# A hybrid decoder layer on one core: x's first 256 columns fetched alone, the first two units by k tiles, the gate weights rounded two units sooner, and one delta order turned

## The reference

```
xn   = RMSNorm(x);  proj = xn @ W_in          (7 x 1024 columns and 16 gate columns b, a)
A    = gated delta rule, 8 heads: conv of 4 taps + SiLU on q, k, v; L2 norm of q, k;
       g = -exp(A_log) softplus(a + dt_bias), beta = sigmoid(b); chunks; RMSNorm * SiLU(z)
B    = block attention, 8 heads, RMSNorm of q and k, causal softmax over the block of 256 keys
h    = x + concat(A, B) @ W_o
h    = h + (silu(RMSNorm(h) @ W_gate) * (RMSNorm(h) @ W_up)) @ W_down       (width 5632)
out  = h + sigmoid(RMSNorm(h) @ W_pg) * (p @ W_pp)                          (p is 256 x 256)
```

## Time and profile before

| | |
|---|---|
| median of three runs | 1342.83 us |
| profiled execution, time / span | 1343.03 us / 1341.0 us |
| DVE busy | 790.0 us (59%) |
| ACT busy | 626.1 us (47%) |
| POOL busy | 53.0 us (4%) |
| matmuls | 6796 |
| DMA, mean | 178 GB/s |

### The profile page before, as it was taken

One profiled execution on the slowest core, in us unless ns is written; L12 is line 12 of the kernel. 1 busy time (PEld: TensorE's weight loads), 2 busy tenths in 40 slices (PEclk: granted clock), 3 DMA queues, 4 the chain that ended last, 5 costly groups with the idle time before them and its releaser, 6 DMA issues.

```text
span 1341.0 us, 18239 instructions
## 1 busy us (share of the span) xinstructions
PE 1333.0 (99%) x6796; PEld 1102.6 (82%) x6796; DVE 790.0 (59%) x987; ACT 626.1 (47%) x785; POOL 53.0 (4%) x71
## 2 busy tenths in 40 slices
PE   9999999999999999999999999999999999999998
PEld 8788888887888888888888888888888888888887
DVE  6578885788586555555555555455555555555554
ACT  6477443543465545444444443344444444444643
POOL 4002000230000000000000000000000000000000
PEclk9999999999999999999999999999999999999999
DMA  8555554455434565666666656666666665555554
GB/s 265 161 170 173 149 150 125 144 153 148 140 120 150 175 194 178 201 190 188 187 189 191 186 189 194 194 191 195 191 194 186 188 189 188 185 189 189 187 192 141
DMA packets 125929, 238.35 MB, mean 178 GB/s; under 512 B 9695, under 2 KB 10258, under 8 KB 125866
## 3 DMA queue, kind: packets, MB, share of 16 engines
q1 hardware_dynamic: 125866, 237.48, 57.9%
HBM read 235.36 MB, written 2.10 MB: 177 GB/s over the span
## 4 chain that ended last, share of the span: by engine, by line
PE 97%; DVE 0%; ACT 0%; issue 0%; DVEq 0%
PE pair L550 30%; PE pair L552 29%; PE pair L551 29%; PE bg L667 2%; PE bg L732 2%; PE bg L815 1%; PE bg L607 1%; PE bg L585 0%; PE bg L713 0%; PE pair L885 0%; PE pair L883 0%; PE pair L884 0%; PE bg L631 0%; PE bg L638 0%; PE bg L647 0%; PE bg L642 0%
## 5 line engine op out<-in xcount | busy, mean ns | idle before, releaser
L1199 DVE TENSOR_TENSOR w_lo<-raw,w_hi 128x1024 fp32r<-128x1024 f32 x443 | 541.6, 1225 | 418.0 <-ACT w_hi L900 414.6
L900 ACT ACTIVATE w_hi<-raw 128x1024 fp32r<-128x1024 f32 x443 | 468.1, 1059 | 486.6 <-PE pair L552 485.1
L550 PE MATMUL pair<-w_hi,xT_hi 128*128 128x512 f32 x1264 | 502.7, 398 | 1.5 <-DVE wba_lo L1447 1.3
L552 PE MATMUL pair<-w_hi,xT_lo 128*128 128x512 f32 x1264 | 492.9, 390 | 0.0
L551 PE MATMUL pair<-w_lo,xT_hi 128*128 128x512 f32 x1264 | 492.4, 390 | 0.0
L552 PEld LDWEIGHTS pair<-w_hi,xT_lo 128*128 128x128 f32 x1264 | 237.3, 188 | 50.5
L550 PEld LDWEIGHTS pair<-w_hi,xT_hi 128*128 128x128 f32 x1264 | 237.4, 188 | 49.6 <-DVE wba_lo L1447 1.4
L551 PEld LDWEIGHTS pair<-w_lo,xT_hi 128*128 128x128 f32 x1264 | 237.6, 188 | 45.9
L550 PE MATMUL pair<-w_hi,actT_hi 128*128 128x512 f32 x352 | 137.7, 391 | 0.0
L552 PE MATMUL pair<-w_hi,actT_lo 128*128 128x512 f32 x352 | 137.1, 389 | 0.0
L551 PE MATMUL pair<-w_lo,actT_hi 128*128 128x512 f32 x352 | 137.0, 389 | 0.0
(11 more groups left out here) (233 smaller groups left out, 880.2 us busy)
## 6 DMA issues: line engine op xcount, KB each, us to landing
raw<-in_w_in_dram SPq DMA_DIRECT2D x112, 512.0 KB, 3.8
raw<-in_w_gate_dram SPq DMA_DIRECT2D x88, 512.0 KB, 4.5
raw<-in_w_up_dram SPq DMA_DIRECT2D x88, 512.0 KB, 3.8
raw<-in_w_down_dram SPq DMA_DIRECT2D x88, 512.0 KB, 4.5
raw<-in_w_o_dram SPq DMA_DIRECT2D x32, 512.0 KB, 4.2
raw<-in_w_ple_gate_dram SPq DMA_DIRECT2D x32, 512.0 KB, 4.5
h<-in_x_dram SPq DMA_DIRECT2D x4, 512.0 KB, 8.3
raw<-in_w_ple_proj_dram SPq DMA_DIRECT2D x4, 512.0 KB, 4.5
```

The source lines that it names most:

```text
L550: mm(banks[t][:], hi[:, ts], wh, start=first, stop=False)
L552: m = mm(banks[t][:], lo[:, ts], wh, start=False, stop=last)
L900: f(w_hi[j % RING][:], raw[j % RING][:], ACT.Copy).then_inc(hi_ready, 1)
L1199: v.tensor_tensor(w_lo[j % RING][:], raw[j % RING][:], w_hi[j % RING][:].bitcast(F32), ALU.subtract).then_inc(lo_ready, 1)
```

## The change

x is fetched in five pieces: 256, 256, 512, 512, 512 columns. The gains' DMA is issued by ACT. The two k tiles of step x 0 go to two banks (the second to `x1_bank`, a bank of the pair that block 1 will use), each with its own semaphore; ACT and DVE then alternate: x k tile 0, unit 0 k tile 0, x k tile 1, unit 0 k tile 1, then step x 1, then unit 1 by k tiles. `ones` is the first tile that POOL sets. The warm-up is 5, 3, and 3 between steps x 0 and x 1, none after. The gate weights are split at unit 5 instead of 7. Where the planner has gramA of chain 1 and a step of chain 0 in one unit, chain 0's comes first.

```diff
@@ -118,13 +118,15 @@
     for u in range(U_QKV + 3 * UPB + 4, U_WO - 1):
+        steps = []
             elif ready and u not in m_units + conv_units:
-                at[u][1].append(chains[c][done[c]])
+                steps.insert(0 if steps and steps[0][0] == "gramA" else len(steps), chains[c][done[c]])
                 done[c] += 1
+        at[u][1] += steps
@@ -161,6 +163,10 @@
     return first, at, banks
+X_PIECES = ((0, CB // 2), (CB // 2, CB), (CB, 2 * CB), (2 * CB, 3 * CB), (3 * CB, D))
+X_PIECE_OF = (0, 1, 2, 2, 3, 3, 4, 4)
@@ -380,18 +388,17 @@
-            def load_x(q):
-                cs = slice(q * CB, (q + 1) * CB)
-                sp.dma_start(h[:, :, cs], x_d[:, :, cs]).then_inc(x_landed[q], 16)
-            sp.dma_start(row_a[:], A["attn_norm"][0].rearrange("(k p) -> k p", p=P)).then_inc(attn_landed, 16)
+            def load_x(n):
+                cs = slice(*X_PIECES[n])
+                sp.dma_start(h[:, :, cs], x_d[:, :, cs]).then_inc(x_landed[n], 16)
                 load(U_QKV + j, j, w_in, KU * (j % UPB), kind * HEADS * P + half * CB)
-                if j in (1, 2, 3):
-                    load_x(j)
+                if j < 4:
+                    load_x(j + 1)
@@ -449,9 +456,9 @@
+            mask(g.memset(ones[:], 1.0))
             mask(g.memset(root[:], 0.5))
-            mask(g.memset(ones[:], 1.0))
@@ -597,14 +604,19 @@
                     if step == "x":
-                        pe.wait_ge(x_landed[b // 2], 16)
+                        pe.wait_ge(x_landed[X_PIECE_OF[b]], 16)
                             k = 2 * b + kk
-                            last = tp(bk[:, kk * TOK + t * P:kk * TOK + t * P + P], h[:, t, k * P:(k + 1) * P], ident[:])
+                            o = x1_bank if (s, kk) == (("x", 0), 1) else bk
+                            m = tp(o[:, kk * TOK + t * P:kk * TOK + t * P + P], h[:, t, k * P:(k + 1) * P], ident[:])
+                            if (s, kk, t) == (("x", 0), 1, NT - 1):
+                                m.then_inc(x1_full, 1)
+                            else:
+                                last = m
@@ -737,13 +749,13 @@
-            pe.wait_ge(masks_ready, 3)
+            pe.wait_ge(masks_ready, 1)
             burst(("x", 0))
+            warm_up(3)
             burst(("x", 1))
-            warm_up(6)
@@ -754,14 +766,16 @@
                     u = U_QKV + n * UPB + j
-                    if u:
+                    if u > 1:
                             wait_read(pe, ("x", j))
-                        if u == 0:
-                            pe.wait_ge(lo_ready if kk else k0_lo, 1)
+                        elif u == 0:
+                            pe.wait_ge(x1_lo, 1)
+                        if u < 2:
+                            pe.wait_ge(lo_ready if kk else k0_lo, u + 1)
@@ -890,7 +904,8 @@
-            act.wait_ge(masks_ready, 1)
+            act.dma_start(row_a[:], A["attn_norm"][0].rearrange("(k p) -> k p", p=P)).then_inc(attn_landed, 16)
+            act.wait_ge(masks_ready, 2)
@@ -924,9 +939,11 @@
                     wait_full(act, s)
-                    for kk in range(2):
+                    if half:
+                        act.wait_ge(x1_full, 1)
+                    for kk in (0, 1) if half is None else (half,):
                         k = 2 * b + kk
-                        f(xT_hi[:, k, :], bk[:, kk * TOK:(kk + 1) * TOK], ACT.Copy,
+                        f(xT_hi[:, k, :], (x1_bank if half else bk)[:, kk * TOK:(kk + 1) * TOK], ACT.Copy,
@@ -1039,19 +1056,25 @@
-                act.wait_ge(x_landed[2 * q], 16)
-                act.wait_ge(x_landed[2 * q + 1], 16)
+                for n in ((3, 4) if q else (0, 1, 2)):
+                    act.wait_ge(x_landed[n], 16)
+            def split_k(u, k):
+                if not k:
+                    act.wait_ge(raw_landed[u], 16)
+                f(w_hi[u][:, k, :], raw[u][:, k, :], ACT.Copy).then_inc(hi_ready if k else k0_hi, 1)
             post("gains", 0)
-            post("x", 0)
+            for k in range(KU):
+                post("x", 0, k)
+                split_k(0, k)
             post("x", 1)
-            act.wait_ge(raw_landed[0], 16)
-            f(w_hi[0][:, 0, :], raw[0][:, 0, :], ACT.Copy).then_inc(k0_hi, 1)
-            f(w_hi[0][:, 1, :], raw[0][:, 1, :], ACT.Copy).then_inc(hi_ready, 1)
-            split(1, 1)
+            for k in range(KU):
+                split_k(1, k)
@@ -1081,7 +1104,7 @@
                             post(*s)
-                    if n == 0 and j == UPB - 1:
+                    if n == 0 and j == 5:
@@ -1216,13 +1239,16 @@
                     col = {"x": G_ATTN, "hA": G_FFN, "hB": G_PLE}[step]
-                    dve.wait_ge(x_hi, hi_base[step] + 2 * b + 2)
-                    for kk in range(2):
+                    dve.wait_ge(x_hi, hi_base[step] + 2 * b + (1 if half == 0 else 2))
+                    for kk in (0, 1) if half is None else (half,):
                         k = 2 * b + kk
-                        m = v.scalar_tensor_tensor(out=xT_lo[:, k, :], in0=bk[:, kk * TOK:(kk + 1) * TOK],
+                        m = v.scalar_tensor_tensor(out=xT_lo[:, k, :], in0=(x1_bank if half else bk)[:, kk * TOK:(kk + 1) * TOK],
                                                    in1=xT_hi[:, k, :].bitcast(F32), op0=ALU.mult, op1=ALU.subtract)
-                    read_out(s, m)
+                    if half:
+                        m.then_inc(x1_lo, 1)
+                    else:
+                        read_out(s, m)
@@ -1408,21 +1434,26 @@
-            post("x", 0)
-            post("x", 1)
-                dve.wait_ge(x_landed[2 * q], 16)
-                dve.wait_ge(x_landed[2 * q + 1], 16)
+                for n in ((3, 4) if q else (0, 1, 2)):
+                    dve.wait_ge(x_landed[n], 16)
-            dve.wait_ge(k0_hi, 1)
-            v.tensor_tensor(w_lo[0][:, 0, :], raw[0][:, 0, :], w_hi[0][:, 0, :].bitcast(F32), ALU.subtract).then_inc(k0_lo, 1)
-            dve.wait_ge(hi_ready, 1)
-            v.tensor_tensor(w_lo[0][:, 1, :], raw[0][:, 1, :], w_hi[0][:, 1, :].bitcast(F32), ALU.subtract).then_inc(lo_ready, 1)
-            split(1, 1)
+            def split_k(u, k):
+                dve.wait_ge(hi_ready if k else k0_hi, u + 1)
+                v.tensor_tensor(w_lo[u][:, k, :], raw[u][:, k, :], w_hi[u][:, k, :].bitcast(F32),
+                                ALU.subtract).then_inc(lo_ready if k else k0_lo, 1)
+            for k in range(KU):
+                post("x", 0, k)
+                split_k(0, k)
+            post("x", 1)
+            for k in range(KU):
+                split_k(1, k)
```

More of the change, by code:

```diff
@@ L279, in build @@
         bg = [bank(f"bg{i}") for i in range(BANKS)]
+        x1_bank = pair[1][0]
         raw_landed = [sem(f"raw_landed{i}") for i in range(RING)]
@@ L286, in build @@
         bank_free = [sem(f"bank_free{i}") for i in range(BANKS)]
-        x_landed, p_landed, attn_landed = [sem(f"x_landed{q}") for q in range(4)], sem("p_landed"), sem("attn_landed")
+        x_landed, p_landed, attn_landed = [sem(f"x_landed{n}") for n in range(len(X_PIECES))], sem("p_landed"), sem("attn_landed")
         small_landed, rows_landed, ba_landed = sem("small_landed"), sem("rows_landed"), sem("ba_landed")
@@ L292, in build @@
         k0_hi, k0_lo = sem("k0_hi"), sem("k0_lo")
+        x1_full, x1_lo = sem("x1_full"), sem("x1_lo")
         gain_s, x_hi, p_hi, ba_hi, ba_lo = sem("gain_s"), sem("x_hi"), sem("p_hi"), sem("ba_hi"), sem("ba_lo")
@@ L900, in split, with post @@
                 f(w_hi[j % RING][:], raw[j % RING][:], ACT.Copy).then_inc(hi_ready, 1)
-            def post(step, b):
+            def post(step, b, half=None):
                 bk, i, use_n = where((step, b))
@@ L953, in post @@
                 elif step == "ct":
-                    kind, half = QKV_BLOCKS[b]
+                    kind, part = QKV_BLOCKS[b]
                     if b:
@@ L959, in post @@
                     for m in range(4):
-                        t0 = kind * HEADS + 4 * half + m
+                        t0 = kind * HEADS + 4 * part + m
                         key = ("ct+" if m > 1 else "ct", b)
@@ L1270, in post @@
                 elif step == "cm":
-                    kind, half = QKV_BLOCKS[b]
+                    kind, part = QKV_BLOCKS[b]
                     for q in range(2):
                         wait_read(dve, ("ct+" if q else "ct", b))
-                        t0 = kind * HEADS + 4 * half + 2 * q
+                        t0 = kind * HEADS + 4 * part + 2 * q
                         v.tensor_tensor(ch[:, t0:t0 + 2, :], mn[q][:].rearrange("p (m n) -> p m n", m=2),
```

## The result

| | median | runs | profiled execution / span |
|---|---|---|---|
| before | 1342.76 us | 1342.41 to 1343.11 (22) | 1343.03 / 1341.0 us |
| changed | 1339.84 us | 1338.8 to 1344.18 (22) | 1340.08 / 1338.0 us |

The ratio is 0.9979, with a 95% interval of 0.9973 to 0.9986: 2.9 us faster, in the profile 3.0 us (spans). The runs of the changed kernel lie much further apart than those of before. One of them took 1344.18 us, 3.5 more than the next; nothing here explains it. The other 21 end at 1340.71.

What follows compares the result with a forecast made beforehand. TensorE, busy 99%, was taken as the bound, so only its waits and start count. Start 1.55, gate weights 1.4 and delta order 0.5 sum to 3.45 us off the median 1342.83, giving 1339.4; range 1338.7 to 1341.0.

Steps and rivals of the forecast that it cites:

- rival 1: Start: weights set the pace, landings don't move or move back; total gain 2.2 to 3.0, say 1340.5; chance 0.13.
- Gate weights, 1.4: Before unit 8: splitting them two units sooner removes TensorE's 1.3 us idle and part of the transposes' latency; 1.4 us.
- Delta order, 0.5: Near 159 us: DVE doing Z1 of pair 0 before gramA of pair 1 removes TensorE's wait for tt; 0.5 us.
- First main matmul at 8.5: Start of the pass: TensorE's first real matmul at 8.5 us instead of 10.34, with ends 8.0 and 9.2.
- the bound of 6.5: Start: earliest landing of unit 0's weights, from 0.45 sooner issue and 0.7 for 256 KB less; 7.0 was taken.
- hidden, up to 1 us of extra delay: Start: gains row issued by ACT lands at about 2.4, TensorE asks no sooner than 3.5, so no cost.
- the sign that the prediction named, that ACT waits for this transfer: Start: ACT's first rounding of weights would wait for their transfer near 7 us.
- The effective start, 1.55: Start through unit 5: the start acts as 8.8 us instead of 10.34, a gain of 1.55 us; ends 0.3 and 2.1.
- moved by 0 to 0.45: Unit 5: its weights, landing at 20.4 us, would move by 0 to 0.45 us.
- The clock: Start: if TensorE's clock rises at 9.85 again, 8.5 to 9.85 loses 0.68 us; gain 1.2 instead of 1.55.
- Rival 4: Units 2 to 5: small stalls keep TensorE at 1.2 GHz, 2.7 us more per unit, slower at 1345.6; chance 0.03.
- Rival 3: Start: transposes delay the clock's rise to 10.5, 2.3 behind work after the last transpose; total 2.75, 1340.1; chance 0.12.

Runs made afterwards that it cites:

- experiment 3: Changed kernel with x's squares (ACT units 2 and 4, DVE units 3 and 5) behind the x step instead of ahead of it; 1339.20 us.
- experiment 6: Changed kernel with the gate weights' DMA issued behind unit 6's weights instead of unit 4's; 1339.40 us.
- experiment 10: Changed kernel with x's squares behind x, gate weights' DMA behind unit 6's, no warm-up between gains and x's first transposes (4 behind them); 1339.28 us.
- experiment 11: Changed kernel with x's squares behind the x step and all warm-up matmuls left out; 1340.34 us.
- experiment 4: Kernel before with only the gate weights split at unit 5 and the delta order turned, start untouched; 1340.58 us.
- experiment 1: Changed kernel with the planner's old delta order at gramA; 1339.89 us.
- experiment 5: Changed kernel with x's squares behind the x step and the planner's old delta order at gramA; 1340.07 us.

## Why the prediction came out as it did

The forecast was 1339.4, the time is 1339.84; the gain 2.9 for 3.45. It lies at the upper end of rival 1 (2.2 to 3.0).

- **Gate weights, 1.4:** the profile has 1.39 between units 6 and 8, undoing it costs 1.33. Right in cause and size; the copies to tq and the bank made no new wait.
- **Delta order, 0.5:** 0.47 us of idle in each of the three profiles with the old order, none with the new; 0.6 in time. Right.
- **First main matmul at 8.5:** 8.41. But two of its inputs were off and cancelled, so the near hit is in part luck. The first weights landed at 6.3, sooner than the taken 7.0 and than the bound of 6.5. The gains' row landed at 3.9 and not at 2.4: "hidden, up to 1 us of extra delay" failed, TensorE waited 0.35 for it, and x's transposes came at 5.57 instead of 5.15. So x's path and not the weights set ACT's first rounding (6.89 for 7.0), and the sign that the prediction named, that ACT waits for this transfer, did not come. The Trainium skill, DMA: Bandwidth & Descriptors, Issuing engines are not separate DMA queues, says that issuing from several engines saves only the sequencer's time, since all share the same DMA engines. It fits: SP's issue came 0.45 us sooner, and the row itself took 3.1 us instead of 1.6.
- **The effective start, 1.55:** this is the term that was mis-sized; it measured 1.05. The step that failed is "moved by 0 to 0.45" for unit 5's landing. It did not come sooner: in the changed kernel's profile it came 0.4 later, at 20.9, and in the nine profiles with the new start and the gate DMA where it was it lies between 19.7 and 21.0, 20.4 in the mean, as before. The chain behind it was priced well (4.35 us, measured 4.4). So s could not act as less than 9.3 (25.3 at unit 5, less 16), which is rival 1's case. What the prediction did not see is unit 4, 0.25 late, though hidden here behind unit 5: ACT rounds x only behind its squares (19.86) there, as DVE does at unit 5. Experiments 3 and 6 each took the stall at unit 5 away.
- **The clock:** a late rise was priced at 0.68 and left out of the forecast. In the changed kernel's profile it put unit 1 off by 0.3, which unit 5 hid; in experiments 6, 10 and 11 it cost 0.85, 1.2 and 2.3, nearly half of the cold time each time, as the step said. Wrong was the moment taken from one profile as if it belonged to the kernel. Rival 4's price of a cold unit, 2.7, was too high: experiment 11 has 2.3, with its matmuls 0.43 us apart and not the 0.46 that doubling 0.23 gives.
- **Rival 3** (the rise stays 2.3 us behind the last transpose): in experiment 4 the rise came ahead of the transposes, in experiment 6 about 1.8 us behind the start of the work after the last of them, in experiment 1 between x's first four and its second four. No such distance holds. **Rival 4:** the small stalls did not make the clock fall in any profile, nor did 1.6 us of idle in experiment 4.

What stays open: what of the spread of the changed kernel comes from the clock and what from landings (unit 5's weights at 19.7 to 21.0 in its relatives, unit 2's at 10.6 to 11.7), and the run of 1344.18.

## What to carry to other kernels

When work at the start is pulled forward, walk every unit behind it to the next slack and ask for each queue what stands ahead of the part it waits for; here about 0.6 us more lay in putting the sums of squares, for which only POOL waits, behind x's step (1339.2 us, faster than both kernels). A sooner issue at the head of a full DMA queue need not bring a landing further down any sooner; here that of unit 5 stayed at 20.4 in the mean. And a start that is bound by ACT and DVE hides when TensorE's clock rises; with less of that cover the runs of this kernel lie 1.9 us apart, where they lay 0.7.

## What the hardware showed beyond that

The moment of the clock's rise is not settled by the kernel. Before and experiment 4 have the same instructions on TensorE up to unit 0, and the rise came at 9.9 in one and 5.4 in the other. Experiments 5 and 6 ran on one chip and have the same start, and there it was 8.2 and 10.4. Over the thirteen profiles with warm-up it lies between 5.4 and 10.4; in the one without it came at 12.7. The Trainium skill, TensorE: Matmul & The Clock Gate, Part 1, says that the monitor runs free of the kernel's start and that the moment varies from run to run. The traces agree that it varies, but by 5 us, where the page has 500 ns to either side. Before, the start depended on it only through the transposes (9.68 or 10.34), which fits its spread of 0.7 us.

2048 pieces of 64 bytes (128 KB) ahead of 512 KB of weights delayed these by 2.1 us (20.9 against 18.8); over all profiles the weights landed at 19.7 to 21.0 with them ahead and at 18.3 to 18.8 without. The next 512 KB of weights, in rows of 2 KB, land only 1.3 us behind (20.9 and 22.2). From 12 to 18 us the queue moved 270 GB/s in the changed kernel and 370 in experiment 6.
